# Seven block products for eight in the mixing's output product, with step-wise norms and a two-part router product

## What is computed

```
h = h + (sigmoid(gA) * yA + sigmoid(gB) * yB) @ W_mix_out     # mixing; W_mix_out is 1024 x 1024
h = h + cross_attention(rms_norm(h, norm_xattn), mem_k, mem_v) # 4 heads, 256 memory tokens, ends in @ w_xo
h = h + hier_moe(rms_norm(h, norm_ffn))                        # group of 4, then top 2 of its 8 experts
y = rms_norm(h, norm_final)
rms_norm(x, g) = x * rsqrt(mean(x * x) + 1e-6) * g
```

## Time and profile before

| what | us |
|---|---|
| median of 3 runs (2243.31 to 2249.68) | 2244.52 |
| the profiled execution's own time | 2251.51 |
| its span, from the first to the last instruction | 2249.8 |
| TensorE busy | 2077.0 (92%) |
| VectorE busy | 674.6 (30%) |
| ScalarE busy | 487.4 (22%) |
| GpSimd busy | 260.0 (12%) |

### The profile page before, as it was taken

How to read it: one execution, slowest core, us unless ns; L and a number is a source line. 1 busy time by engine, 2 the same in 40 slices (tenths; PEclk the granted TensorE clock), 3 DMA queues, 4 the chain that set the end, 5 groups by cost and what they waited for, 6 DMA issues and landing times.

```text
span 2249.8 us, 34395 instructions
## 1 busy us (share of the span) xinstructions
PE 2077.0 (92%) x12922; PEld 1222.5 (54%) x12922; DVE 674.6 (30%) x1599; ACT 487.4 (22%) x1049; POOL 260.0 (12%) x402
## 2 busy tenths in 40 slices
PE   6999988999979999999999999898599999999996
PEld 4577755666644665788887436654333333333332
DVE  5221213666630142333332012533411111111115
ACT  3212212444420100111110112413022222222212
POOL 1001222222223000000000000000011111111110
PEclk9999999999988999999999999999799999999997
DMA  9346777887886112210111110302899999999966
GB/s 323 109 157 197 249 273 259 267 287 261 268 281 240 47 47 78 73 47 26 41 47 66 40 69 28 141 20 99 304 330 384 384 377 367 373 374 372 370 248 236
DMA packets 205069, 458.68 MB, mean 204 GB/s; under 512 B 18721, under 2 KB 44338, under 8 KB 204778
## 3 DMA queue, kind: packets, MB, share of 16 engines
q1 hardware_dynamic: 172330, 357.96, 45.3%
q0 software_dynamic: 32576, 98.53, 12.8%
HBM read 432.51 MB, written 32.17 MB: 207 GB/s over the span
## 4 chain that ended last, share of the span: by engine, by line
PE 84%; DMA 4%; DVE 4%; issue 3%; ACT 2%; SPq 2%; DVEq 1%; POOLq 0%; ACTq 0%; POOL 0%
PE ps L1415 10%; PE ps L961 10%; PE ps L1222 9%; PE ps L970 7%; PE ps L1446 5%; PE ps L1229 5%; PE ps L1426 5%; PE ps L988 5%; PE ps L1088 5%; PE ps L1455 3%; PE ps L1316 2%; PE ps L1003 2%; PE ps L1124 2%; DMA kraw<-in_cache_k 2%; PE ps L1099 2%
## 5 line engine op out<-in xcount | busy, mean ns | idle before, releaser
L961 PE MATMUL ps<-xnT,ring 128*128 128x352 f32 x768 | 232.3, 463 | 0.9 <-ACT xnT L670 0.9
L1415 PE MATMUL ps<-gu,xgT 128*64 128x512 f32 x1024 | 226.8, 595 | 2.9 <-DVE y_b L2470 2.0
L961 PEld LDWEIGHTS ps<-xnT,ring 128*128 128x128 f32 x768 | 146.0, 191 | 88.2 <-issue 9.0
L2566 POOL DMA_DIRECT2D vpage<-in_cache_v x256 | 137.9, 539 | 436.7 <-issue 428.1
L1088 PE MATMUL ps<-consts,kraw 128*128 128x128 f32 x1024 | 141.9, 283 | 28.5 <-DMA kraw<-in_cache_k 18.6
L1088 PEld LDWEIGHTS ps<-consts,kraw 128*128 128x128 f32 x1024 | 115.3, 144 | 61.2 <-issue 30.7
L1998 DVE COPY kt<-ps 128x512 f32<-128x512 f32 x128 | 88.4, 691 | 187.5 <-PE ps L1088 186.6
L1415 PEld LDWEIGHTS ps<-gu,xgT 128*64 128x64 f32 x1024 | 71.1, 137 | 133.5 <-issue 130.4
L1446 PE MATMUL ps<-wd,hidT_a 128*64 128x512 f32 x512 | 118.4, 604 | 18.6 <-ACT hidT_a L1745 11.2
L970 PE MATMUL ps<-ring,mixT 128*128 128x512 f32 (+1 forms) x288 | 124.0, 593 | 1.1 <-DVE mixT L2172 1.1
L1426 PE MATMUL ps<-gu,xgT 128*32 128x512 f32 x1024 | 115.8, 592 | 0.0
(11 more groups left out here) (390 smaller groups left out, 2799.2 us busy)
## 6 DMA issues: line engine op xcount, KB each, us to landing
kraw<-in_cache_k SPq DMA_DIRECT2D x256, 256.0 KB, 3.6
vpage<-in_cache_v POOLq DMA_DIRECT2D x256, 256.0 KB, 4.6
gu<-in_w_expert_gate SPq DMA_DIRECT2D x32, 2048.0 KB, 20.3
gu<-in_w_expert_up SPq DMA_DIRECT2D x32, 2048.0 KB, 24.9
wd<-in_w_expert_down SPq DMA_DIRECT2D x31, 2048.0 KB, 21.2
ring<-in_w_in SPq DMA_DIRECT2D x8, 1024.0 KB, 6.9
yy<-y_d SPq DMA_DIRECT2D x16, 512.0 KB, 9.1
early<-in_w_in SPq DMA_DIRECT2D x6, 1024.0 KB, 10.8
```

Source lines behind the costliest of these rows:

```text
L961: last = nc.tensor.matmul(bank(R.bank(*tag))[:, 0:NC_], slot[:, k, f * P:(f + 1) * P], xnT[:, k, cols_of(n)], start=k == 0, stop=k == KD - 1)
L1415: last = nc.tensor.matmul(bank(0)[h * BA:(h + 1) * BA, :].rearrange("p (x n) -> p x n", x=2), src[:, k, 0:BA], weight[:, k, :, h * DE // 2 ...
L2566: pool.dma_start(vpage[n % VS][:, p, :], t["cache_v"][ds(page, 1)].rearrange("a s d -> (a s) d")).then_inc(v_in[n % VS], 16)
```

## The change

Three edits, in one step.

*Mixing's output product.* Prompt tiles i and i + 4 form a pair. With the features and the output columns halved too, each pair takes seven block products m1 to m7 (4 k-blocks each, 128 x 512) instead of eight. VectorE forms three sums of activations for each pair (four operations of 128 x 512, L2176's kind) and four of weights (128 x 2048), the fourth after the samples' product has read the weights. ScalarE copies m1, VectorE adds the others into the residual, then the input rows. The sample rows take 32 instructions of 32 columns: even and odd k-blocks and the two halves in four column groups of one bank, which VectorE adds. The norm is now a `StepNorm`: ScalarE squares each tile as it is finished, there are two parts (seven tiles, two tiles), and all copies come after the second root.

*Router.* `n_ffn` has three parts and its turns stand between the output products. The logits of tiles 0 to 6 are made in two column groups of one bank, those of tile 7 and the samples after the ninth tile's turn.

*Experts and end.* TensorE's wait ahead of the extra block is gone. The samples come last and are joined by VectorE, each tile's scaling lags two tiles behind its joining, and ScalarE issues one square root before it is needed.

```diff
@@ -286,6 +286,11 @@
...
+        PAIRS = PT // 2
+        row_sum = [[at(f"row_sum{i}{x}", [P, HK, P], w + 8192 + (3 * i + x) * 2048) for x in range(3)] for i in range(PAIRS)]
+        col_sum = [at(f"col_sum{x}", [P, HK, 512], a_norm + x * 8192) for x in range(3)]
+        xa = [at(f"xa{p}", [P, D], w + 8192 + p * 4096) for p in range(4)]
+        junk_xa = at("junk_xa", [P, D], w + 32768)
@@ -354,8 +359,8 @@
...
-        FIN = (PT,) + tuple(range(PT))
-        FIN_PE = (PT, 1, 3, 5)
+        FIN = tuple(range(TILES))
+        FIN_PE = (1, 3, 5)
@@ -552,10 +559,15 @@
...
-        MO = [(0, 0), (1, 0), (0, 1), (1, 1)] + [(i, half) for i in range(2, TILES) for half in range(2)]
-        for i, half in MO:
-            R.add("dve", "mo", i, half)
-        for i in range(TILES):
+        for i in range(PAIRS):
+            R.add("act", "m1", i)
+        R.add("dve", "ms")
+        for i in range(PAIRS):
+            R.add("dve", "m2", i)
+        for i in range(PAIRS):
+            for name in ("m6", "m7", "m5", "m4", "m3"):
+                R.add("dve", name, i)
+        for i in XA_ORDER:
@@ -671,7 +689,65 @@
...
-        n_xat, n_ffn = Norm("nxat", 2, TILES, bufs=xf), Norm("nffn", 3, TILES, bufs=xf)
+        class StepNorm:
...
+            def act_root(self, act, k):
+                part = self.stat[:, self.parts[k][0]:self.parts[k][1]]
+                act.wait_ge(self.mean, k + 1)
+                nc.scalar.activation(part, part, ACT.Sqrt).then_inc(self.root, 1)
...
+            def dve_root(self, dve, k):
+                part = self.stat[:, self.parts[k][0]:self.parts[k][1]]
+                dve.wait_ge(self.squared, self.parts[k][1])
+                nc.vector.tensor_scalar(part, part, 1.0 / D, EPS, ALU.mult, ALU.add).then_inc(self.mean, 1)
+                dve.wait_ge(self.root, k + 1)
+                nc.vector.reciprocal(part, part)
+                dve.drain()
...
+        n_ffn = StepNorm("nffn", 3, H2_ORDER, [(0, 6), (6, 8), (8, 9)], xf, junk)
...
+                    x0 = (i + p * PAIRS) * P
+                    sp.dma_start(xr[p], t["x"][x0:x0 + P, :]).then_inc(xr_in[p], 16)
+            load_inputs(0)
...
-            for i in range(2, TILES):
-                R.read(sp, "mo", i - 2, 1)
-                sp.dma_start(xr[i % 2][0:rows_of(i), :], t["x"][i * P:i * P + rows_of(i), :]).then_inc(xr_in[i % 2], 16)
-            for name in ("xq", "xo"):
-                ring_load(sp, name)
+            R.made(sp, "yc", KD - 1, 1, 1)
+            sp.dma_start(resid[0:NS, PT, :], t["x"][SEQ:NT, :]).then_inc(x_in[PT], 16)
+            ring_load(sp, "xq")
+            for i in range(1, PAIRS):
+                sp.wait_ge(rows_done, 1 + 2 * i)
+                load_inputs(i)
+            ring_load(sp, "xo")
@@ -1252,11 +1335,43 @@
...
-            for i, half in MO:
-                rows_product(("mo", i, half), f"mo{half}", mixT, i, rows_of(i))
-
-            n_xat.pe_turn(pe)
-            R.read(pe, "nxat", TILES - 1, 1)
+            def row_blocks(name, i, left, right):
+                R.pe_free(pe, name, i)
+                for k in range(HK):
+                    last = nc.tensor.matmul(bank(R.bank(name, i)), left[:, k], right[:, k], start=k == 0, stop=k == HK - 1)
+                last.then_inc(R.full, 1)
+            def mixed_rows(i, low):
+                return mixT[:, 0:HK, i * P:(i + 1) * P] if low else mixT[:, HK:KD, i * P:(i + 1) * P]
+            out0, out1 = ring_slot(pe, "mo0"), ring[RING_ORDER.index("mo1") % 2]
+            for i in range(PAIRS):
+                row_blocks("m1", i, mixed_rows(i, True), out0[:, 0:HK])
+            ring_slot(pe, "mo1")
+            R.pe_free(pe, "ms")
+            for k in range(0, KD, 2):
+                for odd in range(2):
+                    for half, weight in enumerate((out0, out1)):
+                        c = (odd * 2 + half) * NS
+                        last = nc.tensor.matmul(bank(R.bank("ms"))[c:c + NS, :], mixT[:, k + odd, SEQ:NT], weight[:, k + odd, :],
+                                                start=k == 0, stop=k == KD - 2)
+            last.then_inc(R.full, 1)
+            for i in range(PAIRS):
+                row_blocks("m2", i, mixed_rows(i, False), out0[:, HK:KD])
+            pe.wait_ge(diffs_ready, 2)
+            for i in range(PAIRS):
+                pe.wait_ge(wsum_ready, KD + i + 1)
+                minus, less, rest = row_sum[i]
+                row_blocks("m6", i, less, col_sum[1])
+                row_blocks("m7", i, minus, col_sum[0])
+                row_blocks("m5", i, mixed_rows(i + PAIRS, True), out1[:, 0:HK])
+                row_blocks("m4", i, mixed_rows(i + PAIRS, False), col_sum[2])
+                row_blocks("m3", i, rest, out1[:, HK:KD])
+            for x in range(TILES):
+                n_xat.pe_turn(pe, x)
+            R.read(pe, "nxat", XA_ORDER[-1], 1)
@@ -1351,29 +1466,57 @@
...
-            for i in H2_ORDER:
+            for x, i in enumerate(H2_ORDER):
...
+                for y in turns_after(x):
+                    n_ffn.pe_turn(pe, y)
...
-            n_ffn.pe_turn(pe)
-            R.read(pe, "nffn", TILES - 1, 1)
+            def logits(place, k, t0, t1, first):
...
+                                        start=k == 0, stop=k == KD - 1)
...
-            for n in range(COLS):
-                R.pe_free(pe, "lgT", n)
-                for k in range(KD):
-                    last = nc.tensor.matmul(bank(R.bank("lgT", n))[0:NG + NE, 0:NC_], wr[:, k, :], xnT[:, k, cols_of(n)],
-                                            start=k == 0, stop=k == KD - 1)
-                last.then_inc(R.full, 1)
-            R.read(pe, "lgT", COLS - 1)
-            turn(("lg",), lambda b: [(b[0:rows_of(i), i * 36:(i + 1) * 36], lgT[:, i * P:i * P + rows_of(i)])
-                                     for i in range(TILES)])
+            R.read(pe, "nffn", H2_ORDER[7], 1)
+            R.pe_free(pe, "lgT", 0)
+            for k in range(KD):
+                logits(0, k, 0, LEFT, 0)
+                last = logits(0, k, LEFT, RIGHT, 64)
+            last.then_inc(R.full, 1)
+            n_ffn.pe_turn(pe, 8)
+            R.read(pe, "nffn", H2_ORDER[8], 1)
+            R.pe_free(pe, "lgT", 1)
+            for k in range(KD):
+                last = logits(1, k, RIGHT, NT, 0)
+            last.then_inc(R.full, 1)
@@ -1506,7 +1649,6 @@
...
-            R.read(pe, "da", LAST - 1), R.read(pe, "db", LAST - 1)
@@ -1681,8 +1823,16 @@
...
-            n_xat.act_stats(act, lambda i: resid[:, i, :], lambda i: R.read(act, "mo", i, 1))
-            n_xat.act_copy(act, xnT)
+            for i in range(PAIRS):
+                copy(("m1", i), resid[:, i, 512:D], lambda b: b)
+            for x in range(TILES):
+                act.wait_ge(rows_done, x + 1)
+                n_xat.act_square(act, x)
+                if x == 6:
+                    n_xat.act_root(act, 0)
+            n_xat.act_root(act, 1)
+            for x in range(TILES):
+                n_xat.act_copy(act, xnT, x)
@@ -1720,10 +1870,33 @@
...
-            n_ffn.act_stats(act, lambda i: resid[:, i, :], lambda i: R.read(act, "h2", i, 1 if i < PT else 0))
-            n_ffn.act_copy(act, xnT)
-            for n in range(COLS):
-                copy(("lgT", n), lgT[:, cols_of(n)], lambda b: b[0:NG + NE, 0:NC_])
+            def square(x):
+                i = H2_ORDER[x]
+                R.read(act, "h2", i, 1 if i < PT else 0)
+                n_ffn.act_square(act, x)
+            for x in range(6):
+                square(x)
+            n_ffn.act_root(act, 0)
+            square(6)
+            for x in range(4):
+                n_ffn.act_copy(act, xnT, x)
+            square(7)
+            n_ffn.act_root(act, 1)
+            for x in (4, 5):
+                n_ffn.act_copy(act, xnT, x)
+            square(8)
+            n_ffn.act_root(act, 2)
@@ -1833,6 +2006,7 @@
...
+            nc.scalar.activation(ss[:, 5, :], ss[:, 5, :], ACT.Sqrt)
@@ -2197,15 +2371,77 @@
...
-            for i, half in MO:
-                r = rows_of(i)
-                if half == 0:
-                    dve.wait_ge(xr_in[i % 2], 16 * (i // 2 + 1))
-                R.made(dve, "mo", i, half)
-                c = slice(half * 512, (half + 1) * 512)
-                nc.vector.tensor_tensor(resid[0:r, i, c], bank(R.bank("mo", i, half))[0:r, :], xr[i % 2][0:r, c],
-                                        ALU.add).then_inc(R.by["dve"], 1)
-            n_xat.dve_scale(dve, lambda i: resid[:, i, :], 3)
+            def row_sums(i):
+                low, high, low_b, high_b = (mixT[:, k:k + HK, x * P:(x + 1) * P] for x in (i, i + PAIRS) for k in (0, HK))
+                minus, less, rest = row_sum[i]
+                nc.vector.tensor_tensor(minus, low, low_b, ALU.subtract)
+                nc.vector.tensor_tensor(low_b, low_b, high_b, ALU.add)
+                dve.drain()
+                nc.vector.tensor_tensor(less, low_b, low, ALU.subtract)
+                dve.drain()
```

(86 more changed lines are left out.)

113 lines of the change are left out of this document (92 added, 21 removed).

## The result

Before 2245.9 us median of four runs (2243.31 to 2249.68), after **2213.47** (2212.26 to 2215.87, four runs): a recorded ratio of **0.9844** with an interval of 0.9825 to 0.9864 (the quotient of the two medians is 0.9856, inside it). The forecast was 2209.6, in a range of 2200 to 2222. The profiled execution took 2212.26, with a span of 2210.5 and a granted clock of 0.968.

A forecast was written before the change was run, and what follows sets the result against it. TensorE, 84% of the chain, was taken as the bound. Terms -24.0 + 4.0 - 10.7 - 1.9 - 2.3 = -34.9 us, from the median of 2244.5, gave 2209.6 us, range 2200 to 2222.

The forecast's parts named there:

- The product: Mixing's output product: 224 block instructions and cheap sample rows, 100.0 us in place of 124.0, 24.0 less.
- Rival (1): Mixing's product: VectorE's sums come late and TensorE waits 15 us before m6, 2225 us; chance 0.09.
- The norm: Mixing product's end to query product: copies held behind the second root, 20.7 us for 16.7, 4.0 more.
- Router: Output product and router: turns between output products give VectorE all logits at 59.8 instead of 70.5, 10.7 us less.
- Product 7 ends at 32.7: Output products ahead of the router: this one waits about 1 us for ScalarE's first copy, then ends at 32.7 us.
- rival (2): Experts: DMA limits, only the weights' earlier start passes on, router's 10.7 becomes 6.4, 2214 us; chance 0.13.
- Extra block: Extra expert block: TensorE loses its wait for the last results' readers, 1.9 us less.
- Joining and last norm: Kernel's end: samples last, last scaling 39.8 us after the loads' start instead of 41.4, smaller last store, 2.3 less.
- Rival (3): Samples or unequal logit parts: column groups do not run side by side, 2225 us; chance 0.04.
- Rival (4): Mixing's norm costs 8 us more, not 4, and query product starts at low clock, 2.5 more, 2216; chance 0.08.
- Rival (5): Slower than before: clock stays at 1.2 GHz into the query product, 114 us for 57.08, 2267; chance 0.02.
- Rival (6): Better: norm costs no more than before and the tail 4 us less than forecast, 2202 us; chance 0.05.

The follow-up runs named there:

- the later series: Last of three run series, on its own chip, with the unaltered changed kernel beside three altered ones: changed kernel 2218.49 us, ratio 0.987 to the kernel before.
- sums_longer: Changed kernel with mixing's first weight difference computed nine times over, 19 us more on VectorE: 2230.37 us, ratio 0.9913 to the kernel before.
- after_again: Changed kernel unaltered, run again on another chip: 2218.49 us, ratio 0.987 to the kernel before.
- scaled_early: Changed kernel with early copies in mixing's norm and the router's, and mixing's first root and four scalings between the pairs: 2203.5 us, ratio 0.9786.
- mix_only: Kernel before with only the mixing's output product and its norm changed: 2227.07 us, ratio 0.9909.
- end_only: Kernel before with only the order of the joining and the last norm changed, including the early square root: 2244.34 us, ratio 0.9983.
- router_copies_early: Changed kernel with ScalarE's copies of turned tiles moved ahead of squares in the norm before the router: 2206.37 us, ratio 0.983 to the kernel before.
- router_only: Kernel before with only the norm ahead of the router, the router's product and its copies changed: 2238.03 us, ratio 0.9956.
- weights_late: Changed kernel with the experts' first weight loads held until the first logits: 2215.9 us, two runs, ratio 0.9853 to the kernel before.

## Why the prediction held, step by step

The total was forecast at -34.9 us and came at -32.4 by the medians. The difference, 2.5 us or 0.1%, is less than the runs resolve, and the terms measured in the trace make 34.9 as well. That the sum is met to the tenth is luck: the errors cancel (product 0.2 short, norm 1.05 better, router 1.3 short, the end 0.3 better), and it comes from one profile each. In the later series the medians give 29.6.

*The product*, 24.0 forecast, 23.8 measured. 224 x 0.431 = 96.5 held (14.00 + 82.61 us for 224 instructions), the samples' 3.6 was 3.57. The Trainium skill (TensorEngine Tiling (Array Packing), Key Properties) says that a change of tiling mode drains TensorE. The trace has room for little of it: m1 and the samples together are 0.2 us over 32 x 0.431 + 3.6. The sums were to end 7 to 9 us early and ended 11.1 early: 2.29 us each, at the lower of the two bounds. Rival (1), late sums, did not happen, and sums_longer confirms the cover: 11 of its 19 added microseconds did not show.

*The norm*, +4.0 forecast, +2.95 measured. The mechanism, all copies behind the second root, is the right one, and early copies took 2.4 back. The size was off by 1 us: the copies began 11.4 us behind the product's end (forecast 12.1) and took 8.2 (forecast 8.6). The pace of the turns played no part: in after_again the last 40 turns ran at the full clock and were done 1.6 us earlier, and the query product still began 19.65 us behind the product. Nor was the second root the whole cost: scaled_early brought another 5 us by not starting the scaling behind the last pair.

*Router*, 10.7 forecast (logits at 59.8), 9.4 measured (60.9). Here a step failed: "Product 7 ends at 32.7", which has it at 7 us after a wait of 1. It ended at 34.4: the wait was 1.28, but the low clock after it (1.8 us) was not foreseen; the text placed the low clock only behind the 2.6 us of idling ahead of the logits. There it came in three profiles (8.4 to 8.5 us) and stayed away in four (7.03), so that the 8.5 counted for the logits fitted this execution's 8.38 is partly luck. Nor is 9.4 the gain of every pair of executions: the router's product of the kernel before took 16.09 us in its own profile and 14.39 in mix_only and end_only, where the same code runs. With the low clock on both sides, the first expert comes 9.4 us earlier (108.8 to 99.4), with the full clock on both 8.0 to 8.5 (106.4 and 106.9 to 98.4). router_copies_early shows the price of the wait ahead of product 7 together with that of the longer one ahead of the logits: 5.6 to 6.5 us to the first expert. That the whole gain passes on to the experts, against rival (2), held: router_only gave 9.9, and weights_late shows that the loads had time to spare.

*Extra block*, 1.9 forecast, 2.0 measured. *Joining and last norm*: forecast 39.8 us from the loads' start to the last scaling and 2.3 less in all; measured 39.5 and, to the span's end, 2.6 less. Not foreseen was one wait of VectorE for an output buffer whose store was not done (1.09 us at 2196.01). What the earlier square root gives was not tried by itself.

Rival (3), column groups that don't run side by side, did not happen, but is not impossible: it happens in part once their instructions stand in line. Rival (4) had nothing of its first half (the norm cost 2.95 more, not 8) and a little of its second: 1.5 us of low clock in the query product of some executions, for its 2.5. Rival (5) got no support: where the query product had the low clock at all, it cost 1.5 to 1.7 us. Rival (6), norm no worse than before, needed other code: scaled_early has a norm of 12.1 us for the 16.7 before and, with the router's early copies, 2203.5 in all.

## What to carry to other kernels

Where an engine works strictly in order, look for what stands ahead of the work that the bounding engine waits for: copies behind squares on ScalarE cost 5.6 to 6.5 us here, by 1.3 and 1.8 us of waiting and by low clock behind it (1.8 us, and 1.35 more in some executions), while eight more wide operations on VectorE cost nothing for their first 11 us. Give column groups their instructions in turn, not group by group. A term of 2 us is read from a trace, counted from a mark inside the stage: neither medians nor the difference of two whole spans resolve it.

## What the runs showed of the hardware, not expected

The granted clock fell after waits that were short. After 1.28 us of idling behind 32 turns at 1.00, it went down to 0.50 in product 7, in every one of the seven profiles with that wait. After 2.69 us ahead of the logits it fell in three profiles of seven, with the same instructions in front of it.

The query product looks like a second case of that kind: 57.08 us in the changed kernel's first profile, 58.53 in after_again, from the same code, with starts 0.03 us apart. But what stands in front of it differs. TensorE's timelines, the first profile, then after_again:

```profile
1330.31 6.22 PE L746 MATMUL ps<-consts,xa 128*128 128x128 f32 x40 [2.11 <-ACT xnT L719]
1338.21 7.07 PE L1044 MATMUL ps<-xnT,ring 128*128 128x352 f32 x23 [1.68 <-ACT xnT L719]
```
```profile
1330.28 4.66 PE L746 MATMUL ps<-consts,xa 128*128 128x128 f32 x40 [1.90 <-ACT xnT L719]
1338.18 7.04 PE L1044 MATMUL ps<-xnT,ring 128*128 128x352 f32 x18 [3.25 <-ACT xnT L719]
```

In the first, the last 40 turns began at the low clock and took 6.22 us; TensorE then waited 1.68 us for ScalarE's copies, and the query product ran at 1.00. In the second the turns ran at the full clock and took 4.66 us; TensorE waited 3.25 us, and the product began at 0.50. The stretches of the product's start, in the same order:

```profile
1336.00:1346.00 10.00, 8.32 (x31) 5.33 (x30) 0.00 (x0) 2.62 (x6) 0.00 (x0) 1.00 0.00 0
```
```profile
1336.00:1346.00 10.00, 7.82 (x22) 4.94 (x23) 0.00 (x0) 2.60 (x6) 0.00 (x0) 0.83 0.00 0
```

Over the seven profiles with this norm unaltered: the wait of 1.68 us (three profiles) was never followed by the low clock, that of 3.25 us in three of four (58.5 to 58.8 us; router_copies_early has it and 57.08). So turning fast gained nothing, as the copies set the start, and the longer idling that it left was followed by a slower product in most cases. Why not in the fourth is open, and the length of the wait alone does not decide: in scaled_early 1.80 us of it, behind turns at 1.00, was followed by 58.77 us.

The first expert's product did likewise, 7.09 us in the first profile and 10.02 in after_again, with the same waits in front of it. Of the two executions of one kernel, after_again thus lost 4.4 us in these two products and had 1.35 back in the logits, 3.0 in all, with no edit made.
